# First projection tiles fed from a transposed copy of x

## The reference

```python
def rms_norm(x, g):
    xf = x.astype(jnp.float32)
    y = xf * lax.rsqrt(jnp.mean(xf * xf, axis=-1, keepdims=True) + EPS)
    return (y * g.astype(jnp.float32)).astype(x.dtype)

def mamba2_layer(x, norm_g, w_in, conv_w, conv_b, dt_bias, a_log, d_skip, gate_norm_g, w_out):
    h = rms_norm(x, norm_g)
    zxbcdt = h @ w_in
    ...
    xbc = jax.nn.silu(causal_depthwise_conv(xbc, conv_w, conv_b))
    ...
    dt = jax.nn.softplus(dt_raw.astype(jnp.float32) + dt_bias.astype(jnp.float32)).reshape(b, s, G, R)
```

## Time and profile before

| | |
|---|---|
| time, median of 3 | 1227.38 us (1225.37 to 1227.44) |
| the profiled execution's own time | 1224.2 us |
| its span | 1222.5 us |
| PE busy | 1205.7 us, 99% of the span |
| DVE, ACT, POOL busy | 906.3, 668.0, 52.1 us |
| first projection product | 11.14 us after the span's start |
| DMA | 115.42 MB, 94 GB/s on average |

### The profile page before, as it was taken

How to read it: one execution, slowest core, us unless ns; L and a number is a source line. 1 busy time by engine, 2 the same in 40 slices (tenths; PEclk the granted TensorE clock), 3 DMA queues, 4 the chain that set the end, 5 groups by cost and what they waited for, 6 DMA issues and landing times.

```text
span 1222.5 us, 18051 instructions
## 1 busy us (share of the span) xinstructions
PE 1205.7 (99%) x6649; PEld 1002.8 (82%) x6649; DVE 906.3 (74%) x1399; ACT 668.0 (55%) x1093; POOL 52.1 (4%) x46
## 2 busy tenths in 40 slices
PE   8999999999999999999999999999999999899997
PEld 6788888888888887878787899747889888899886
DVE  5888889888965366777677789997777424786776
ACT  6666756675653244555655563684667312577222
POOL 1011210121010000000000000000000000000000
PEclk9999999999999999999999999999999999999999
DMA  6433333423324232222222223114333233232322
GB/s 172 139 95 114 91 99 103 120 81 108 103 69 146 87 91 82 70 70 76 78 69 69 70 87 87 52 52 121 86 104 104 86 101 122 69 104 89 119 88 103
DMA packets 169099, 115.42 MB, mean 94 GB/s; under 512 B 3392, under 2 KB 162400, under 8 KB 168016
## 3 DMA queue, kind: packets, MB, share of 16 engines
q1 hardware_dynamic: 167152, 104.02, 28.9%
q0 software_dynamic: 1888, 10.62, 2.5%
HBM read 112.46 MB, written 2.16 MB: 94 GB/s over the span
## 4 chain that ended last, share of the span: by engine, by line
PE 93%; DVE 3%; ACT 1%; DMA 1%; issue 1%; SPq 0%; ACTq 0%; DVEq 0%
PE psum L650 53%; PE psum L1183 10%; PE psum L1272 6%; PE psum L920 4%; PE psum L852 4%; PE psum L1026 3%; PE psum L1081 2%; PE psum L889 2%; PE psum L907 1%; PE psum L756 1%; PE psum L764 1%; PE psum L747 1%; PE psum L901 1%; PE psum L738 1%; PE psum L732 1%
## 5 line engine op out<-in xcount | busy, mean ns | idle before, releaser
L1308 ACT ACTIVATE w_hi<-w_raw 128x1024 fp32r<-128x1024 f32 x158 | 166.8, 1056 | 279.6 <-PE psum L650 203.7
L1978 DVE TENSOR_TENSOR w_lo<-w_raw,w_hi 128x1024 fp32r<-128x1024 f32 x158 | 193.0, 1222 | 111.2 <-ACT w_hi L1308 110.6
L650 PE MATMUL psum<-a_hi,w_hi 128*128 128x512 f32 (+1 forms) x656 | 233.4, 376 | 0.2
L650 PE MATMUL psum<-a_lo,w_hi 128*128 128x512 f32 (+1 forms) x656 | 228.7, 368 | 0.0
L650 PE MATMUL psum<-a_hi,w_lo 128*128 128x512 f32 (+1 forms) x656 | 227.8, 367 | 0.0
L650 PE MATMUL psum<-b_hi,w_hi 128*128 128x512 f32 x376 | 149.9, 399 | 0.0
L650 PE MATMUL psum<-b_lo,w_hi 128*128 128x512 f32 x376 | 148.5, 395 | 0.0
L650 PE MATMUL psum<-b_hi,w_lo 128*128 128x512 f32 x376 | 148.0, 394 | 0.0
L650 PEld LDWEIGHTS psum<-a_hi,w_hi 128*128 128x128 f32 x656 | 118.3, 188 | 24.7 <-issue 3.9
L650 PEld LDWEIGHTS psum<-a_hi,w_lo 128*128 128x128 f32 x656 | 118.1, 188 | 21.4
L650 PEld LDWEIGHTS psum<-a_lo,w_hi 128*128 128x128 f32 x656 | 118.0, 188 | 19.7
(11 more groups left out here) (398 smaller groups left out, 2504.9 us busy)
## 6 DMA issues: line engine op xcount, KB each, us to landing
w_raw<-a_w_in SPq DMA_DIRECT2D x48, 512.0 KB, 3.9
w_raw<-w_down SPq DMA_DIRECT2D x32, 512.0 KB, 3.8
arena<-acs POOLq DMA_DIRECT2D x8, 1024.0 KB, 5.1
w_raw<-a_w_out SPq DMA_DIRECT2D x16, 512.0 KB, 4.0
w_raw<-w_kv SPq DMA_DIRECT2D x16, 512.0 KB, 3.7
w_raw<-b_w_in SPq DMA_DIRECT2D x16, 512.0 KB, 3.9
w_raw<-w_in SPq DMA_DIRECT2D x14, 512.0 KB, 3.8
arena<-w_up SPq DMA_DIRECT2D x7, 1024.0 KB, 5.3
```

Source lines behind the costliest of these rows:

```text
L650: ins = mm(out, wv[:, u.par, k, :], xv[:, k0 + k, c0:c0 + cn], start=(first and begin and i == 0 and n == 0), stop=(last and end and i == ...
L1308: ac(w_hi[:, u.par, :, :], w_raw[:, u.par, :, :], ACT.Copy).then_inc(S["hi_ready"], 1)
L1978: tt(w_lo[:, u.par, :, :], w_raw[:, u.par, :, :], f32(w_hi[:, u.par, :, :]), ALU.subtract).then_inc(S["lo_ready"], 1)
```

## The change

A second input holds x transposed on the host, features first (`x_t`). SP fetches tile 0's weights first, then `x_t` straight into `h` in four pieces of two feature blocks, then tile 1's weights, the time-step weights, the identity, all of x with tokens in partitions in one transfer of 2 MB (a semaphore of its own, `tok_in`), then tile 2's weights and so on.

PE transposes nothing of x. It warms with 14 products in place of 4 (and 2 between the pieces of x). `a_hi` and `a_lo` are made from `h`, and the copies to `h` are gone. The spreading of the norm's factor moves from tile 1 to tile 2, behind its first six blocks (`SPREAD = 6`). ACT squares two blocks of tokens, makes tile 2's high half, then squares the other two. The six tiles of the first group go to PSUM banks 1, 0, 3, 2, 1, 0, so tiles 2 and 3 don't wait for tiles 0 and 1 to be read. On DVE, the low half of tile 2's weights now stands before the inversion.

```diff
+FIRST_BANKS = (1, 0, 3, 2, 1, 0)
+WARM = 14
+SPREAD = 6
...
+            load(Lin(U_MAMBA), t["a_w_in"], 0, ssd_cols(Lin(0))[0])
+            for i in range(4):
+                sp.dma_start(h[:, 2 * i:2 * i + 2, META:T2], t["x_t"].rearrange("(k p) s -> p k s", p=P)
+                             [:, 2 * i:2 * i + 2, :]).then_inc(S[f"x_in{i}"], 16)
+            load(Lin(U_MAMBA + 1), t["a_w_in"], 0, ssd_cols(Lin(0))[1])
+            sp.dma_start(wdt, t["w_dt"]).then_inc(S["raw0"], 16)
             sp.dma_start(ident, t["consts"][:, K_ID:K_ID + P]).then_inc(S["con_in"], 16)
-
-            for i in range(4):
-                if i == 1:
-                    load(Lin(U_MAMBA), t["a_w_in"], 0, ssd_cols(Lin(0))[0])
-                if i == 3:
-                    sp.dma_start(wdt, t["w_dt"]).then_inc(S["raw0"], 16)
-                sp.dma_start(x_tok[:, :, 256 * i:256 * i + 256], t["x"].rearrange("(t p) d -> p t d", p=P)
-                             [:, :, 256 * i:256 * i + 256]).then_inc(S[f"x_in{i}"], 16)
-
-            group(Lin(0), 1)
+            sp.dma_start(x_tok, t["x"].rearrange("(t p) d -> p t d", p=P)).then_inc(S["tok_in"], 16)
+
+            group(Lin(0), 2)
...
-            warm(4).then_inc(S["unit_done"], 1)
-            pe.wait_ge(S["con_in"], 16)
-
-            def turn_x(ks):
...
-            for k in (0, 2, 4):
-                turn_x((k, k + 1))
-                if k < 4:
-                    warm(1)
+            warm(WARM).then_inc(S["unit_done"], 1)
...
             u, m = Lin(U_MAMBA), Lin(M_MAMBA)
-            tile_of(u, m, a_hi, a_lo, False, ks=range(2), ready=("x_lo", 1))
-            turn_x(range(6, KT))
-            tile_of(u, m, a_hi, a_lo, False, ks=range(2, KT), ready=("x_lo", 3))
+            tile_of(u, m, a_hi, a_lo, False, ready=("x_lo", 1))
             u, m = u + 1, m + 1
             tile_of(u, m, a_hi, a_lo, False, ks=range(3))
             pe.wait_ge(S["dtw_ready"], 1)
             dt_products()
             tile_of(u, m, a_hi, a_lo, False, ks=range(3, 5))
-            pe.wait_ge(S["rs_ready"], 1)
-            spread(bank(4), stat_at(X_RS), TOKENS1, S["rb_ready"])
             tile_of(u, m, a_hi, a_lo, False, ks=range(5, KT))
...
             def first_group(j, ks=range(KT)):
-                tile_of(Lin(U_MAMBA + j), Lin(M_MAMBA + j), a_hi, a_lo, False, ks=ks)
+                tile_of(Lin(U_MAMBA + j), Lin(M_MAMBA + j), a_hi, a_lo, False, ks=ks,
+                        free=M_MAMBA if j < 4 else M_MAMBA + j - 3, out=bank(FIRST_BANKS[j]))
...
-            first_group(2)
+            first_group(2, range(SPREAD))
+            pe.wait_ge(S["con_in"], 16)
+            pe.wait_ge(S["rs_ready"], 1)
+            spread(bank(4), stat_at(X_RS), TOKENS1, S["rb_ready"])
+            first_group(2, range(SPREAD, KT))
...
-            turned_high((0, 1))
             hi(Lin(U_MAMBA))
-            turned_copies((1,))
-            turned_high((2, 3, 4, 5))
-            for i in range(4):
-                act.wait_ge(S[f"x_in{i}"], 16)
-            token_squares(0)
-            turned_high((6, 7))
+            turned_high(range(KT))
             hi(Lin(U_MAMBA + 1))
-            turned_copies((3, 5, 7))
-            for i in range(1, NT):
+            act.wait_ge(S["tok_in"], 16)
+            for i in range(2):
+                token_squares(i)
+            hi(Lin(U_MAMBA + 2))
+            for i in range(2, NT):
                 token_squares(i)
             act.wait_ge(S["xsum_ready"], NT)
             own.wait()
             root(stat_at(X_SD), stat_at(X_SUM), eps1, 1.0 / D, S["xsd_ready"])
-            hi(Lin(U_MAMBA + 2))
...
-            turned_low((0,))
-            turned_copies((0,))
-            turned_low((1,))
             lo(Lin(U_MAMBA))
-            turned_low(range(2, KT))
+            turned_low(range(KT))
             lo(Lin(U_MAMBA + 1))
...
-            turned_copies((2, 4, 6))
...
-            dve.wait_ge(S["xsd_ready"], 1)
-            nc.vector.reciprocal(stat_at(X_RS), stat_at(X_SD)).then_inc(S["rs_ready"], 1)
...
             lo(Lin(U_MAMBA + 2))
+            dve.wait_ge(S["xsd_ready"], 1)
+            nc.vector.reciprocal(stat_at(X_RS), stat_at(X_SD)).then_inc(S["rs_ready"], 1)
             dve.wait_ge(S["rt_ready"], 1)
...
-        "x": x["x"][0], "a_w_in": x["a_w_in"][0], "a_w_out": x["a_w_out"][0], "w_kv": x["w_kv"],
+        "x": x["x"][0], "x_t": x["x"][0].T, "a_w_in": x["a_w_in"][0], "a_w_out": x["a_w_out"][0], "w_kv": x["w_kv"],
```

More of the change, by code:

```diff
@@ L353, in build @@
             "pool_ready poolm_ready yf_ready yh_ready yl_ready half_hi half_lo "
-            "lam_sum lam_exp sp_pre sp_exp "
+            "lam_sum lam_exp tok_in sp_exp "
             "ft_ready fh_ready fl_ready left_add left_sq left_ready right_add right_done osum_ready ors_ready left_done left_end out_done").split():
@@ L580, in _ @@
             pool.wait_ge(S["xsum_ready"], NT)
-            pool.wait_ge(S["x_tp"], KT)
             def spread(g):
@@ L629, in tile_of @@
             def tile_of(u, m, xh, xl, wide, k0=0, first=True, last=True, ks=range(KT), ready=None,
-                        begin=None, end=None, lo="lo_ready", free=None, mark=None):
+                        begin=None, end=None, lo="lo_ready", free=None, mark=None, out=None):
                 begin = ks[0] == 0 if begin is None else begin
@@ L643, in tile_of @@
                 else:
-                    outs = [(acc(m), 0, SEQ)]
+                    outs = [(acc(m) if out is None else out, 0, SEQ)]
                 for i, k in enumerate(ks):
@@ L648, in tile_of @@
                     for n, (wv, xv) in enumerate(((w_hi, xh), (w_hi, xl), (w_lo, xh))):
-                        for out, c0, cn in outs:
-                            ins = mm(out, wv[:, u.par, k, :], xv[:, k0 + k, c0:c0 + cn],
+                        for o, c0, cn in outs:
+                            ins = mm(o, wv[:, u.par, k, :], xv[:, k0 + k, c0:c0 + cn],
                                      start=(first and begin and i == 0 and n == 0),
@@ L681, in _, with dt_products @@
             pe.wait_ge(S["warm_set"], 1)
-            warm(4).then_inc(S["unit_done"], 1)
-            pe.wait_ge(S["con_in"], 16)
-            def turn_x(ks):
-                for k in ks:
+            warm(WARM).then_inc(S["unit_done"], 1)
+            def dt_products():
+                for k in range(KT):
                     if k % 2 == 0:
                         pe.wait_ge(S[f"x_in{k // 2}"], 16)
[L690 to L701, removed]
                     c = slice(32 * (k % 4), 32 * (k % 4) + 32)
@@ L816, in _ @@
             pe.wait_ge(S["dt_tok"], 1)
-            pe.wait_ge(S["x_cpa"], 4)
             pe.wait_ge(S["tab_in"], 16)
@@ L1321, in turned_high @@
                 for k in ks:
-                    act.wait_ge(S["x_tp"], k + 1)
-                    ac(a_hi[:, k, 0:SEQ], bank(2 + k % 6), ACT.Copy,
+                    act.wait_ge(S[f"x_in{k // 2}"], 16)
+                    ac(a_hi[:, k, 0:SEQ], h[:, k, META:T2], ACT.Copy,
                        scale=par[:, C_ANORM + k:C_ANORM + k + 1]).then_inc(S["x_hi"], 1)
[L1326 to L1329, removed]
             def token_squares(i):
@@ L2016, in turned_low @@
                     dve.wait_ge(S["x_hi"], k + 1)
-                    stt(a_lo[:, k, 0:SEQ], bank(2 + k % 6), par[:, C_ANORM + k:C_ANORM + k + 1],
+                    stt(a_lo[:, k, 0:SEQ], h[:, k, META:T2], par[:, C_ANORM + k:C_ANORM + k + 1],
                         f32(a_hi[:, k, 0:SEQ]), ALU.mult, ALU.subtract).then_inc(S["x_lo"], 1)
[L2020 to L2023, removed]
-            turned_low((0,))
-            turned_copies((0,))
-            turned_low((1,))
             lo(Lin(U_MAMBA))
-            turned_low(range(2, KT))
+            turned_low(range(KT))
             lo(Lin(U_MAMBA + 1))
@@ L2062, in evacuate_in @@
                 n, m = g * 6 + j, g * 6 + (M_MAMBA + j)
+                v = bank(FIRST_BANKS[j]) if g.reg is None and g.c == 0 else acc(m)
                 if j == 0:
@@ L2068, in evacuate_in @@
                         dve.wait_ge(S["pre_silu"], (g * 4 + j).v)
-                    tt(pre[:, 3:3 + SEQ], acc(m), rt[:, 0:SEQ], ALU.mult).then_inc(S["acc_read"], 1)
+                    tt(pre[:, 3:3 + SEQ], v, rt[:, 0:SEQ], ALU.mult).then_inc(S["acc_read"], 1)
                     return
                 dve.wait_ge(S["silu_done"], (n - 1).v)
-                tt(conv[:, j % 2, :], acc(m), rt[:, 0:SEQ], ALU.mult).then_inc(S["acc_read"], 1)
+                tt(conv[:, j % 2, :], v, rt[:, 0:SEQ], ALU.mult).then_inc(S["acc_read"], 1)
             def taps_of(g, j):
```

## The result

The changed kernel takes 1234.19 us (median of 5, 1233.31 to 1234.58), the kernel before beside it 1227.38 (1225.37 to 1229.22): a ratio of 1.0057, with a 95% interval of 1.0044 to 1.0071. It is 6.8 us slower. The profiled execution took 1233.97 us, span 1232.3.

The account below looks back on a forecast made before the run. The prediction took PE (93% of the chain) as the bound, with DVE's chain to tile 3's low half as late. Tile 3's delay 3.8 plus clock 2.2 made 6.0 us on 1227.4: 1233.4 us, range 1229.2 to 1236.8.

Parts of the forecast that it names:

- The landing of x_tok: Transfer of x with tokens in partitions: all landed at 19.3 us, ends 18.3 and 21.2.
- the first term: Start of tile 3: 35.85 us against 32.03, so 3.8 us later, waiting for DVE's low half.
- PE before T: PE's start: tile 0 near 9.7 us in place of 11.1, PE through at 23.2 where before 26.33.
- T: The time when all of x with tokens in partitions has landed, taken as 19.3 us.
- Tile 2, the spreading, the row: Tile 2 starts at T + 4.6 = 23.9, spreading at T + 8.8 = 28.1, row `rt` at T + 10.1 = 29.4 us.
- PE and not x holds the spreading: In tile 2: factor inverted about T + 6, but PE reaches the spreading behind 18 products, at T + 8.8 = 28.1 us.
- DVE's chain: DVE's work from the row `rt` to tile 3's low half: 6.3 us, low half ready at T + 16.4 = 35.7.
- The clock: PE's clock falls in the 5.9 us wait before tile 3, costing 2.2 us more, ends 0 and 3.3.
- Nothing gives it back: Behind tile 3, DVE's and PE's work both shift by the same 3.8 us, and no later part recovers it.
- The median: Base of the forecast: 1227.4 us, the median of three runs, 3.2 us above the profiled execution's 1224.2.
- The rival in which the clock stays up: At the wait before tile 3 the clock does not fall: +3.8 us, 1231.2, chance 0.25.
- The faster rival: Tile 3's low half is ready when PE ends tile 2, at 29.9, 2.1 us sooner: 1225.3, chance 0.07.

Follow-up runs that it names:

- the late spreading alone: The kernel before with only the four banks and the spreading moved behind six blocks of tile 2, x still turned on PE: 1234.66 us, ratio 1.0066.
- the run that kept PE at work: The changed kernel with 26 products of the identity with itself, which nothing reads, between tiles 2 and 3: 1232.0 us.
- idle products in both: The kernel before with 9 and 15 unread identity products in PE's two feed-forward waits (near 902 and 1042 us): 1224.77 us, ratio 0.9980.

## Why the prediction was right

It said 1233.4, and it was 1234.19. Term by term:

- **The landing of x_tok.** 19.3 predicted; ACT's first square began at 19.88. Too early by 0.6 us: the long rows moved at 376 GB/s and not 390 from 14 to 18 us, and at 252 from 18 to 20. That is the miss in the first term, 4.3 in place of 3.8. The prediction also misread what the Trainium skill's figure gives: 358 GB/s for both transfers makes, in its own sum, 14.0 + 5.9 - 0.1 = 19.8, which is 0.5 us and not 0.9 later than 19.3. This estimate from the page DMA: Bandwidth & Descriptors, section Bandwidth, is near the measured 19.88, but 358 was no limit here: x_tok moved at 376 GB/s for four microseconds. The same section says that the figure is each core's share when both cores of an HBM domain stream, and lists 425 GB/s for a transfer of 16 MB with the other core idle; this kernel runs on one core, and the trace agrees in that it passes 358.
- **PE before T.** Tile 0 was to start at 9.7 and started at 10.43. The slow stretch of the warming products lasted longer than in the profile of before. So the 0.7 us that PE was to wait before tile 2 did not come: PE was through at 24.41, just as the low half let tile 2 start (24.43, 4.55 us behind the first square as in the other runs). It cost nothing; the run with ten warming products started tile 2 the same 4.54 us behind the first square.
- **Tile 2, the spreading, the row.** T + 4.6, T + 8.8 and T + 10.1 were 24.5, 28.7 and 30.0 by the first square, and 24.43, 28.83 and 30.00 measured. That the spreading's place counts was shown both ways: SPREAD = 2 took back 3.5 to 4 us, the late spreading alone cost 7.7. The sentence that PE and not x holds the spreading is half the truth. PE reaches it behind six blocks of a tile that x_tok itself holds back, so the landing moves all three times, as the letter T in them says.
- **DVE's chain.** 6.3 predicted, 6.19 measured.
- **The clock.** 2.2 predicted, 2.48 measured, and the run that kept PE at work brought the time-step products 2.3 us sooner. The size was right in part by luck. The one fall on record came 5.2 us after PE had stopped, which in a wait of 5.9 left little room; here it came after 4.2. The slow stretch lasted 5.4 us of PE's work and not 4.5. For the upper end of 3.3 the prediction gives no working, and the terms of its high end add up to 1236.4, not 1236.8.
- **Nothing gives it back.** The shift of 6.8 at the time-step products is still 6.8 at 303 us of the kernel before. The two chains, before and after:

```profile
303.28 0.87 PE psum L732 x8
```

```profile
310.07 0.87 PE psum L712 x8
```

- **The median.** Here the working had a hole. I added 6.0 to the median without saying why that lay 3.2 above the profiled execution. The two later waits explain most of it: the profiled execution had both free of a fall, and with idle products in both the median is 2.35 us lower. That the median execution has one or two falls is worked out from this and from 1.5 us for each; no profile of such an execution of the kernel before was taken. The change's own loss of 6.5 to 6.8 holds with and without them, so the forecast was not hurt.

The rival in which the clock stays up was wrong for this kernel, and its reason too: a wait of 3.46 us that does nothing in one execution is no proof. The next one was followed by a fall, as was one of 2.89. The faster rival asked for DVE to be through in half a microsecond, and it needed 6.19.

## What to carry to other kernels

When a stage is made to start sooner, follow each row of the next engine's order to the first thing that PE needs, and see what it stands behind. A step that many wait for (here four small transposes) belongs at the first point where its input is there, not at a convenient one. If that place is behind work that itself waits for a late transfer, the two delays add up. And a wait of PE of some microseconds can cost more than its length; if it can't be removed, products on data that nobody reads can be worth their place.

## What the runs showed of the hardware

I had not expected waits as short as these to cost the clock, and not in some executions only. A wait of 3.46 us left it up in one profile and was followed by a fall in another, 2.89 us was followed by one, and so was 2.00 us, behind which the clock fell when PE was at work again. Waits of 1.19 and 0.67 us left it up. A fall after a short wait cost about 1.5 us: 1.56 behind the 2.89 us, and 3.0 for the two later ones of the changed kernel together (9.8 - 6.8). That at tile 3 cost 2.5. The clock fell 2.1 us after PE's last product in the run with tile 3's halves ahead of the row, 4.2 in the changed kernel, 4.7 in the run with the late spreading and 5.2 at the end of the kernel before. What sets the moment I did not find out. The scatter of the kernel before (1224.3 to 1229.7 over the sets) goes with the mean granted clock of the run: its run at 1224.27 had 0.999, those near 1225.7 had 0.997 or 0.998, those near 1227.0 had 0.996, and those near 1229 had 0.994 or 0.995. The Trainium skill, TensorE: Matmul & The Clock Gate, section HAM oscillation, says that PE which waits for its data between bursts of products starts the next burst at the lower clock. The trace agrees at tile 3, where a wait of 5.67 us came before and 2.48 us were lost; the wait of 3.46 us that left the clock up shows that it is not so for each wait.
